# Other start addresses for the activation and weight buffers of the fp32r matrix products

## What is computed

```python
q, k, v = jnp.split(h @ w_qkv, 3, axis=-1)          # layer 0
q, v, g, f_fwd, f_bwd = jnp.split(h @ w_in, splits, axis=-1)   # layer 1
return (jax.nn.silu(a) * u) @ w_out                 # feed-forward, layers 0 and 1
proj = h @ w_in                                     # hybrid layers
...
merged = jax.nn.sigmoid(ga) * (y_att @ w_proj_attn) + jax.nn.sigmoid(gr) * (y_ret @ w_proj_ret)
return x + gate[:, None, :] * (merged @ w_out)
```

## Time and profile before

| | |
|---|---|
| runs | 3481.1, 3481.22, 3482.25 us; median 3481.22 us |
| span of the profiled execution (first to last instruction) | 3481.5 us |
| PE busy | 3315.7 us, 95% |
| PEld busy | 2746.0 us, 79% |
| DVE / ACT / POOL busy | 1704.4 / 1290.2 / 397.6 us |
| share of PE in the chain that ended last | 80% |
| DMA | 318.75 MB, 92 GB/s on average |
| mean granted TensorE clock | 0.983 of 2.4 GHz |

### The profile page before, as it was taken

How to read it: one execution, slowest core, us unless ns; L and a number is a source line. 1 busy time by engine, 2 the same in 40 slices (tenths; PEclk the granted TensorE clock), 3 DMA queues, 4 the chain that set the end, 5 groups by cost and what they waited for, 6 DMA issues and landing times.

```text
span 3481.5 us, 42896 instructions
## 1 busy us (share of the span) xinstructions
PE 3315.7 (95%) x17064; PEld 2746.0 (79%) x17064; DVE 1704.4 (49%) x2596; ACT 1290.2 (37%) x1994; POOL 397.6 (11%) x400
## 2 busy tenths in 40 slices
PE   4999989999999999988999999999999999999998
PEld 3788877888887877876888878887778788877786
DVE  3666667655524676766433334343343333434433
ACT  2555543212123556464322333333332333333422
POOL 1111110000001354442000000000100000011000
PEclk7999999999999999999999999999999999999999
DMA  5222223666521111111333232222223222222232
GB/s 181 78 81 77 77 72 120 195 193 203 184 80 58 60 47 51 43 45 62 97 97 97 85 105 73 67 85 79 70 74 99 98 78 74 67 85 79 62 94 87
DMA packets 109286, 318.75 MB, mean 92 GB/s; under 512 B 28192, under 2 KB 30880, under 8 KB 108576
## 3 DMA queue, kind: packets, MB, share of 16 engines
q1 hardware_dynamic: 109088, 316.00, 29.0%
HBM read 313.86 MB, written 2.10 MB: 91 GB/s over the span
## 4 chain that ended last, share of the span: by engine, by line
PE 80%; DVE 7%; ACT 4%; POOL 4%; issue 2%; DMA 1%; SPq 1%; DVEq 0%; ACTq 0%
PE bank L1060 20%; PE bank L1064 20%; PE bank L1061 20%; PE bank L1071 3%; PE bank L1075 3%; PE bank L1072 3%; PE bank L1280 1%; PE bank L1154 1%; PE bank L1164 1%; DVE w_low L1712 1%; POOL hg_d L2215 1%; PE bank L1299 1%; PE bank L1309 1%; PE bank L1181 1%; POOL hg_d L2212 1%
## 5 line engine op out<-in xcount | busy, mean ns | idle before, releaser
L1060 PE MATMUL bank<-h_high_lat,w_high 128*128 128x512 f32 x2742 | 1129.1, 412 | 57.9 <-ACT h_high_lat L1341 24.3
L1064 PE MATMUL bank<-h_low_lat,w_high 128*128 128x512 f32 x2742 | 1080.5, 394 | 1.4 <-DVE h_low_lat L1774 1.4
L1061 PE MATMUL bank<-h_high_lat,w_low 128*128 128x512 f32 x2742 | 1078.3, 393 | 0.0
L1712 DVE TENSOR_TENSOR w_low<-w_raw,w_high 128x1024 fp32r<-128x1024 f32 (+3 forms) x442 | 541.4, 1225 | 1056.4 <-ACT w_high L1360 1055.4
L1360 ACT CAST w_high<-w_raw 128x1024 fp32r<-128x1024 f32 (+3 forms) x442 | 451.8, 1022 | 1247.1 <-PE bank L1064 821.6
L1060 PEld LDWEIGHTS bank<-h_high_lat,w_high 128*128 128x128 f32 x2742 | 521.3, 190 | 167.1 <-issue 74.2
L1064 PEld LDWEIGHTS bank<-h_low_lat,w_high 128*128 128x128 f32 x2742 | 519.2, 189 | 120.9 <-DVE h_low_lat L1774 9.7
L1061 PEld LDWEIGHTS bank<-h_high_lat,w_low 128*128 128x128 f32 x2742 | 522.0, 190 | 80.5 <-issue 7.7
L2169 POOL TENSOR_TENSOR rstd<-rstd,square 128x512 f32<-128x512 f32 (+1 forms) x42 | 65.5, 1560 | 1424.1 <-ACT square L1341 1423.1
L1075 PE MATMUL bank<-h_low_ctx,w_high 128*128 128x256 f32 x795 | 225.4, 284 | 0.1
L1072 PE MATMUL bank<-h_high_ctx,w_low 128*128 128x256 f32 x795 | 225.1, 283 | 0.0
(11 more groups left out here) (264 smaller groups left out, 4368.4 us busy)
## 6 DMA issues: line engine op xcount, KB each, us to landing
w_raw<-in_w_in_dram SPq DMA_DIRECT2D x176, 512.0 KB, 3.5
w_raw<-in_ada_w_dram SPq DMA_DIRECT2D x88, 512.0 KB, 3.8
w_raw<-in_ffn_in_dram SPq DMA_DIRECT2D x88, 512.0 KB, 3.6
w_raw<-in_w_ada_dram SPq DMA_DIRECT2D x48, 512.0 KB, 4.3
w_raw<-in_hg_in_dram SPq DMA_DIRECT2D x40, 512.0 KB, 3.5
w_raw<-in_ffn_out_dram SPq DMA_DIRECT2D x32, 512.0 KB, 3.5
w_raw<-in_qkv_dram SPq DMA_DIRECT2D x24, 512.0 KB, 3.6
w_raw<-in_proj_ret_dram SPq DMA_DIRECT2D x16, 512.0 KB, 3.6
```

The lines of the kernel that those rows point to most:

```text
L1060: e.matmul(lat_b, a, h[:, k, :], start=start, stop=False)
L1061: e.matmul(lat_b, b, h[:, k, :], start=False, stop=False)
L1064: done = e.matmul(lat_b, a, l[:, k, :], start=False, stop=stop)
L1712: e.tensor_tensor(w_lo[n % 2][:, 0:w], raw[slot][:, 0:w], w_hi[n % 2][:, 0:w].bitcast(F32), ALU.subtract).then_inc(s_lo, 1)
```

## The change

It changes the order of the declarations and adds two paddings. No instruction, wait or DMA is added, removed or moved; only the addresses in them change. The lines of the engine code stand 6 lines further down.

```diff
         cm = sb("matrices", [P, 5, P])
-        vec = sb("vectors", [P, NVEC])
         XL = sb("x_lat", [P, KC, LAT])
-        HhL, HlL = sb("h_high_lat", [P, KC, LAT], F32R), sb("h_low_lat", [P, KC, LAT], F32R)
+        HhL = sb("h_high_lat", [P, KC, LAT], F32R)
+        RAW_N = 3
+        raw = ring("w_raw", RAW_N, [P, KC * P])
+        w_hi0 = sb("w_high0", [P, KC * P], F32R)
+        HlL = sb("h_low_lat", [P, KC * LAT + 8], F32R)[:, 4:4 + KC * LAT].rearrange("p (k t) -> p k t", t=LAT)
+        w_lo0 = sb("w_low0", [P, KC * P], F32R)
+        sb("line_pad", [P, 24])
+        w_hi1 = sb("w_high1", [P, KC * P], F32R)
+        lbs = sb("lower_bound", [P, 2, 16])
+        w_lo1 = sb("w_low1", [P, KC * P], F32R)
+        w_hi, w_lo = [w_hi0, w_hi1], [w_lo0, w_lo1]
         RS = sb("rstd", [P, TOK])
         sqr = ring("square", 2, [P, TOK])
         tmp = ring("tmp", 2, [P, TOK])
-        RAW_N = 3
-        raw = ring("w_raw", RAW_N, [P, KC * P])
-        w_hi, w_lo = ring("w_high", 2, [P, KC * P], dt=F32R), ring("w_low", 2, [P, KC * P], dt=F32R)
+        vec = sb("vectors", [P, NVEC])
...
-        lbs = sb("lower_bound", [P, 2, 16])
```

## The result

The kernel before took 3481.73 us in this comparison (3481.1 to 3482.62, 4 runs), the changed one 3503.07 us (3501.86 to 3504.5, 4 runs). The ratio is 1.0063, with a 95% interval of 1.0051 to 1.0075: 21 us slower. Forecast were 3449 us, a gain. The three lat products are now L1066, L1067 and L1070 (1060, 1061 and 1064 before).

The account below looks back on a forecast made before the run. The prediction took TensorE's issue of fp32r matmuls to bound the kernel. Terms of -8, -12 and -12 us, the rest 0, summed to -32 us, from 3481 to 3449 us; range 3385 to 3535, likeliest case 3425 to 3474.

Parts of the forecast that it names:

- What bounds the kernel, and the only way to move it: Whole kernel: TensorE's matmul issue sets the time; only the same instruction taking another time at another address can move it.
- Lat products on `h_*`, -8 us: 8226 matmuls on three lines: 1 ns of settling gained on each, steady pitch unchanged; -8 us.
- The 1 ns of settling: Matmuls on `h_*_lat`: part of the 4 ns between mean and median record, taken as gained 8226 times.
- Lat products on the other buffers, -12 us: 2016 matmuls on the other lat buffers: reach the pitch of `h_*`, 6 ns less each; -12 us.
- Context products, -12 us: 2913 context matmuls: fall to the shortest record in the trace, 4 ns less each; -12 us.
- All others, DVE, ACT and DMAs at 0: Other matmuls, VectorE, ScalarE and DMAs: no loss to address today, or any cost hidden; 0 us.
- the lock is lost: Rival, 36%: `h_*` matmuls lose equal offsets with their weights and go to 233.3 ns; +46 to +55 us, 3488 to 3537 us.
- The record that it named as its sign: Median record of lat matmuls on `h_*` at 394 ns or more would show the slower outcome.
- Its point of decision: The slower rival decides as soon as the pitch on `h_*` rises by 2.9 ns.
- The bare stream: Rival, 15%: new offsets remove half or all of the 13 ns lost per `h_*` matmul; 3311 to 3425 us.
- Weights have nothing to do with it: Rival, 12%: weight offsets do not matter and the address matters little; no change, 3481 +- 7 us.

Follow-up runs that it names:

- e2: The kernel before with only the four weight buffers moved, from offset 192 to 128: 3495.17 us, ratio 1.0040.
- m1: Bench without the network's arithmetic: 39 streams of 48 fp32r matmuls, one moving and one weight buffer each at varied offsets; settled pitch 226.7 ns at difference 0.
- m2: Bench of 31 streams repeating one chunk's products at a layout's offsets, 24 of them mixing lat and context matmuls; equal offsets modulo 256 settled at 226.7 ns.
- e6: The changed kernel with `w_high1` and `w_low1` at the first pair's offsets, 128 and 160: 3507.28 us, ratio 1.0079.
- e8: The kernel before with only `w_high1` and `w_low1` moved, to offsets 320 and 448: 3498.39 us, ratio 1.0053.
- e5: The kernel before with one 64-byte pad, putting `u2_*`, `ya_*`, `yr_*` and `m_*` at offset 192 like their weights: 3473.59 us, ratio 0.9974.
- e1: The kernel before with every moving and weight buffer of the products at offset 128: 3481.05 us, ratio 0.9996.
- m3: Bench: six streams alternating two matmuls on equal weights and two on weights at another offset, then 15 mixed streams; pitches 226.8 to 232.8 ns in five of the six.

## Why the prediction was wrong

**What bounds the kernel, and the only way to move it**: right. The time moved by 21.3 us, TensorE's busy time by 21.1, with no other engine taking part and TensorE's idle time shorter by 2.5 us.

**Lat products on `h_*`, -8 us**: the step that failed. "I leave the steady pitch where it is" took 226.7 ns to be something that these products keep at any address. They had it because `h_*` and all their weights were equal modulo 256 (e2, m1). In the change two of the six products still are (`h_high_lat` with `w_high0`, and with `w_low1`, 256 bytes away), and that does not save even these: one unequal buffer lengthens the whole stream (m2). Measured: 227.9 to 231.3 ns, +22.4 us by the three groups, +21.9 by the starts. The first pair's pattern in all pieces costs +27 us (e6), the second pair's in half of them +18 (e8). The 1 ns of settling that was to be gained was not: in pieces without a context the pitch stays at 231 to 232 ns to their end.

**Lat products on the other buffers, -12 us**: the same mistake from the other side. "I take them to the pitch that `h_*` has" is what happens where they get equal offsets: -9.2 us by the starts in e5 for the 1488 late matmuls. In the change they lie at 256 beside weights at 128, 160, 256 and 384; only the products on `w_high1` are equal. The late ones gained 1.0 ns, 1.5 us in all, nearly all of it on pair 1 (231.3 ns against 233.1 on pair 0).

**Context products, -12 us**: they kept their median of 281 ns. The shortest record of a group was not what this layout gave: the 2913 records became 2 us shorter together, their starts 0.4 us farther apart. In alternation with lat matmuls the offsets of both count together (m2), so they have no price of their own.

**All others, DVE, ACT and DMAs at 0**: right; the casts take 1225 and 1021 ns, as before.

So the sum of -32 us had its size from gains that did not come, and nothing in it for the loss that did: by the starts +21.9 on `h_*` against -8, -1.8 on the other lat buffers against -12, +0.4 on the context against -12.

**The rival "the lock is lost"** had the mechanism, and was given 36%. It was priced with one entry of the table, 233.3 ns, for all pairs: +46 to +55 us. The change's two patterns, run by themselves, cost 231.2 ns (m2, `d` and `e`), and the kernel lost about half of that sum; 3503 us lies in the lower band that it kept for a part of the products being hit, though here all three products were hit, each by less. The record that it named as its sign, 394 ns, was not reached either (393). Its point of decision, a rise by 2.9 ns, was passed at 3.4. Its objection, that "unequal is slow" was a single case, was sound as to the size. The bare stream did not come: no steady stream of any run was below 226.6 ns. Its 213.3 ns were taken from the earlier trace rows, where a plain float32 matmul of 512 columns stands as two records with starts 428.5 ns apart, 1.8 ns over 2 cycles a column; that fp32r could have as little over its one cycle was a guess, and even equal offsets leave 13.3 ns over.

**"Weights have nothing to do with it"** is refuted by e2, which moves only the weights (and small tables), and by m1. The reading taken there from the Trainium skill (TensorE: Matmul & The Clock Gate, What happens when you issue a matmul; SBUF — State Buffer, Who interferes with whom), two independent read ports and so no effect of the relation of the offsets, does not agree with these runs: the relation is worth 226.7 against 233.3 ns. Whether it is a port that makes it so, no run here shows. Rows 7 had pointed in its favour, and what they show stands: also a matmul without a weight load beside it keeps the length of its set. Over the whole trace of before there are 32 such on `h_low_lat`, at a median of 388 ns, and 5 on the late buffers, all at 397; in e5 these 5 have 388. So it is not simply a collision with the next load. (The ends of matmul records are modelled, so this is weaker than a difference of starts.)

**What the trace of before would have allowed.** The two sets in the earlier trace rows differ in two ways, in the moving offset and in its relation to the weights. Nothing in them says which one counts. The forecast took the better value for every layout, the rival the worse one for every unequal pair; both counted offsets modulo 512, where 256 is the period. A price for "some of six buffers unequal" could not be had from it.

**Open.** The rule is shown, its mechanism is not: why the pitch has this order of offsets, why equal is good and 64 nearly so, and why even equal offsets leave 13.3 ns over one cycle a column. Why a stream needs time to come down (eleven matmuls in the earlier trace rows, about six at the mean of the 14 such changes of buffer and on the bench). Why mixed streams of 512 and 256 columns have another best pair than pure ones, and another on the bench than in the kernel. Not tried: a pair of weight buffers for the context products alone, and other offsets for `h_*_ctx` in the kernel e5, which is where e1's loss suggests that time is left or lost. Nor `u_*` with weights as in e8's second pair, 14 ns a chunk better there.

## What to carry to other kernels

In dense streams of fp32r matmuls of 512 columns the moving buffer and the weight buffers should start at the same offset modulo 256 bytes, high and low parts and both buffers of a double buffer alike; here that was worth 6.7 of 233.3 ns a matmul, and one unequal buffer in the pattern took most or all of it (16 bytes on one of three: 5.3 ns, 32 bytes: all). So a small array declared among the large ones is a change of timing: after any edit of the declarations compare the median record per moving buffer, and try a pad of 64 bytes before a rewrite. Where products of different widths alternate, measure the layout in the kernel itself, since neither the equal layout nor the bench's best one was the best there.

## What the runs showed of the hardware

- The pitch of an fp32r matmul of 512 columns at the full clock depends on the start addresses of its two operands: 226.7, 228.9, 232.3 to 232.7 and 233.3 ns for (moving - weights) modulo 256 of 0, 64, 128 and 192, for three places of the moving buffer, with one exception in 24 pairs (m1).
- The single matmul does not have a pitch of its own by its own offsets: with two equal and two unequal members in turn all four took 229.8 to 235.3 ns (m3). The settled sums over a chunk in m2 are mostly multiples of 6.67 ns, 16 cycles of 2.4 GHz (680.0, 693.3, 700.0).
- Prices don't add: an offset of 32 bytes on one buffer of three gives 233.2 ns, with one of 16 on another besides it gives 231.2 (m2).
- Streams that alternate 512 and 256 columns have other best offsets: in e1, with all equal, their chunks on `h_*` took 1053.2 ns against 1040.3 before.
- VectorE's and ScalarE's casts, whose operands moved by the same steps, did not change: 1225 and 1021 ns against 1225 and 1022 (the earlier trace rows and the rows above).
